# Attention scores of one head at a time over all 128 array rows, with zero-padded q, in place of two heads side by side in two row tiles

## The reference, cut to what matters

```python
h = rms_norm(x, attn_norm)
qa, ka, va, qd, kd, vd = split(h @ w_in)            # 256 x 512 each
qa, ka, qd, kd = rope of each, in 8 heads of 64 columns
out_a = rms_norm(merge_heads(moba_attention(qa, ka, va)))
out_d = rms_norm(merge_heads(dilated_attention(qd, kd, vd)))
x = x + concatenate([out_a, out_d]) @ w_out
x = x + square(relu(rms_norm(x) @ w_up)) @ w_down   # d_ff 4096
# inside the attention, for every head:  scores = q @ k.T * 64 ** -0.5
```

## Time and profile before

| | |
|---|---|
| median of 3 runs | 613.45 us (613.41 to 613.94) |
| the profiled execution's own time | 614.13 us |
| its span in the trace | 612.0 us |
| mean granted TensorE clock | 0.998 |
| PE busy | 600.8 us, 98% |
| DVE, ACT, POOL busy | 62%, 52%, 7% |

### The profile page before, as it was taken

How to read it: one execution, slowest core, us unless ns; L and a number is a source line. 1 busy time by engine, 2 the same in 40 slices (tenths; PEclk the granted TensorE clock), 3 DMA queues, 4 the chain that set the end, 5 groups by cost and what they waited for, 6 DMA issues and landing times.

```text
span 612.0 us, 8795 instructions
## 1 busy us (share of the span) xinstructions
PE 600.8 (98%) x3145; PEld 500.2 (82%) x3145; DVE 378.7 (62%) x576; ACT 316.5 (52%) x534; POOL 44.2 (7%) x42
## 2 busy tenths in 40 slices
PE   7999999999999999999999999999999999999995
PEld 4788787888888888888888788788888888888884
DVE  4854854588675665656388355737976565655734
ACT  5746567656443534534184545764763544535423
POOL 1220140010000000000004010400100000000001
PEclk9999999999999999999999999999999999999999
DMA  8954234328746556465256443422586556466201
GB/s 304 344 206 139 99 116 131 135 73 274 261 156 219 188 168 239 142 232 180 69 189 224 139 137 139 123 84 70 182 297 215 199 155 242 151 198 214 103 0 69
DMA packets 58952, 104.05 MB, mean 170 GB/s; under 512 B 1792, under 2 KB 35376, under 8 KB 58928
## 3 DMA queue, kind: packets, MB, share of 16 engines
q1 hardware_dynamic: 58576, 103.19, 49.8%
q10 hardware_dynamic: 352, 0.55, 0.3%
HBM read 102.69 MB, written 1.05 MB: 170 GB/s over the span
## 4 chain that ended last, share of the span: by engine, by line
PE 94%; DMA 2%; DVE 1%; issue 1%; POOL 1%; ACT 1%; SPq 1%; POOLq 0%; DVEq 0%; ACTq 0%
PE psum L921 19%; PE psum L795 19%; PE psum L797 18%; PE psum L796 18%; PE psum L924 10%; DMA raw<-in_w_in 2%; PE psum L865 2%; PE psum L802 1%; PE psum L856 1%; PE psum L881 1%; PE psum L882 1%; PE psum L901 1%; PE psum L897 1%; PE psum L880 1%; POOL roped L343 1%
## 5 line engine op out<-in xcount | busy, mean ns | idle before, releaser
L529 DVE TENSOR_TENSOR w_lo<-raw,w_hi 128x1024 fp32r<-128x1024 f32 x190 | 231.0, 1251 | 53.0 <-ACT w_hi L385 53.0
L385 ACT CAST w_hi<-raw 128x1024 fp32r<-128x1024 f32 x190 | 188.5, 1047 | 3.7 <-DMA raw<-in_w_in 3.0
L921 PE MATMUL psum<-xt,w_hi 128*128 128x512 f32 x512 | 160.8, 395 | 0.0
L795 PE MATMUL psum<-w_hi,ot_hi 128*128 128x512 f32 x320 | 127.0, 397 | 0.0
L797 PE MATMUL psum<-w_hi,ot_lo 128*128 128x512 f32 x320 | 124.8, 390 | 0.0
L796 PE MATMUL psum<-w_lo,ot_hi 128*128 128x512 f32 x320 | 124.7, 390 | 0.0
L924 PEld LDWEIGHTS psum<-xt,w_lo 128*128 128x128 f32 x512 | 96.2, 188 | 22.4
L924 PE MATMUL psum<-xt,w_lo 128*128 128x256 f32 x512 | 100.6, 278 | 0.0
L921 PEld LDWEIGHTS psum<-xt,w_hi 128*128 128x128 f32 x512 | 80.2, 189 | 2.3
L795 PE MATMUL psum<-w_hi,xt 128*128 128x512 f32 x192 | 79.9, 416 | 1.6 <-DVE w_lo L529 1.0
L476 ACT COPY up_cross<-psum 128x512 f32<-128x512 f32 x32 | 18.8, 587 | 118.9 <-PE psum L924 118.9
(11 more groups left out here) (79 smaller groups left out, 472.5 us busy)
## 6 DMA issues: line engine op xcount, KB each, us to landing
raw<-in_w_up SPq DMA_DIRECT2D x32, 1024.0 KB, 5.5
raw<-in_w_down SPq DMA_DIRECT2D x32, 1024.0 KB, 6.8
raw<-in_w_in SPq DMA_DIRECT2D x22, 1024.0 KB, 5.5
raw<-in_w_out SPq DMA_DIRECT2D x8, 1024.0 KB, 4.8
raw<-in_w_in SPq DMA_DIRECT2D x2, 512.0 KB, 5.1
raw<-in_w_in SPq DMA_DIRECT2D x3, 256.0 KB, 3.6
out<-x SPq DMA_DIRECT2D x3, 256.0 KB, 2.4
x<-in_x SPq DMA_DIRECT2D x2, 256.0 KB, 4.1
```

Source lines behind the costliest of these rows:

```text
L385: act.copy(w_hi[:, slot, part], raw[:, slot, part]).then_inc(hi_done, 1)
L529: dve.tensor_tensor(w_lo[:, slot, part], raw[:, slot, part], w_hi[:, slot, part].bitcast(F32), ALU.subtract).then_inc(split_done, 1)
L795: pe.matmul(out, s_hi, m_hi, start=first, stop=False)
L921: pe.matmul(up_banks[b][:, f, :], w_hi[:, slot, cols[f]], xt[:, k, :, :].rearrange("p a b -> p (a b)"), start=k == 0, stop=False)
```

## The change

Head 2n and head 2n+1 of a pair are no longer computed in two row tiles. The array `q_t` becomes `q_pad`, with two copies of each tile: copy 0 has head 2n's q in partitions 0 to 63 and zeros in the others, copy 1 has head 2n+1's q in partitions 64 to 127 and zeros in the others. Each of the four matmuls of a pair then uses all 128 rows, with `k_t` of both heads as the moving operand, and the zeros cancel the other head's part. They stand in another order: both matmuls of the even head, then both of the odd one. Each ACT copy of q out of `t_bank` becomes two, one for each half of the partitions. DVE sets `q_pad` to zero once at the start, and ACT waits for that once.

```diff
-        q_t = sb("q_t", [4, SEQ])
+        q_pad = sb("q_pad", [2, 4, SEQ])
...
+        zeros_set = sem("zeros_set")
...
                         n = QKT_AT[s]
-                        dst = (q_t, k_t)[n // 2 % 2]
+                        tiles = slice(2 * (n % 2), 2 * (n % 2) + 2)
                         act.wait_ge(qk_turned, l * 8 + n + 5)
-                        act.copy(dst[:, 2 * (n % 2):2 * (n % 2) + 2, :],
-                                 t_bank[:, :].rearrange("p (a b) -> p a b", a=2)).then_inc(qk_copied, 1)
+                        if n // 2 % 2 == 0:
+                            lower, upper = slice(0, HEAD_DIM), slice(HEAD_DIM, P)
+                            if l == 0 and n == 0:
+                                act.wait_ge(zeros_set, 1)
+                            act.copy(q_pad[lower, 0, tiles, :],
+                                     t_bank[lower, :].rearrange("p (a b) -> p a b", a=2))
+                            act.copy(q_pad[upper, 1, tiles, :],
+                                     t_bank[upper, :].rearrange("p (a b) -> p a b", a=2)).then_inc(qk_copied, 1)
+                        else:
+                            act.copy(k_t[:, tiles, :],
+                                     t_bank[:, :].rearrange("p (a b) -> p a b", a=2)).then_inc(qk_copied, 1)
...
             dve.memset(squares[:, 1, 0:BANK], 1.0).then_inc(ones_set, 1)
+            dve.memset(q_pad[:, :, :, :], 0.0).then_inc(zeros_set, 1)
...
                     if hh >= 2:
                         pe.wait_ge(masked, l * N_HEADS + h)
-                    lower, upper = slice(0, HEAD_DIM), slice(HEAD_DIM, P)
                     n = hh // 2
-                    pe.matmul(s_banks[0][:, 0:P], q_t[lower, n, 0:P], k_t[lower, n, 0:P],
-                              start=True, stop=True)
-                    pe.matmul(s_banks[1][:, 0:P], q_t[upper, n, 0:P], k_t[upper, n, 0:P],
-                              start=True, stop=True)
-                    pe.matmul(s_banks[0][:, P:3 * P], q_t[lower, n, P:2 * P], k_t[lower, n, :],
-                              start=True, stop=True).then_inc(scored, 1)
-                    pe.matmul(s_banks[1][:, P:3 * P], q_t[upper, n, P:2 * P], k_t[upper, n, :],
-                              start=True, stop=True).then_inc(scored, 1)
+                    for e in range(2):
+                        pe.matmul(s_banks[e][:, 0:P], q_pad[:, e, n, 0:P], k_t[:, n, 0:P],
+                                  start=True, stop=True)
+                        pe.matmul(s_banks[e][:, P:3 * P], q_pad[:, e, n, P:2 * P], k_t[:, n, :],
+                                  start=True, stop=True).then_inc(scored, 1)
```

## The result

| | before | changed |
|---|---|---|
| median, us | 613.98 (6 runs) | 618.39 (6 runs) |
| lowest to highest | 613.41 to 614.71 | 617.75 to 618.75 |
| ratio | | 1.007, 95% interval 1.0059 to 1.0082 |
| span of the profiled execution | 612.0 | 616.3 |
| PE busy | 600.8 | 605.2 |

The changed kernel is slower by 4.4 us, 0.7%. The forecast was +4.2, and 618.39 lies within its range.

What follows compares the result with a forecast made beforehand. PE was taken to bound the kernel. Pairs +4.3, copies +0.1 and given back −0.2 summed to +4.2 us: 618.3 us for the profiled execution (617.7 on the median), range 615.9 to 619.7, 84%.

Steps and rivals of the forecast that it cites:

- The bound: Whole kernel: PE is busy 600.8 of 612.0 us, so more or less streaming on PE is kernel time.
- The two switches: Scores of each pair: entering and leaving row tiles goes away, saving 0.40 us a pair, 6.4 us in all.
- Streaming: Scores: heads run one after the other, 1.32 us a pair against 1.05; +0.27 a pair, +4.3 us (+3.4 to +5.8).
- the border of up to 0.04: Scores: 0.04 us a pair for entering and leaving full-array float32, counted in the upper bound of 1.41 a pair.
- Copies: Eight q copies on ACT become sixteen; PE gets `t_bank` back later in slot 13 of both layers: +0.1 us (0.0 to 0.3).
- Zeros: Start of the kernel: DVE's zeroing ends at 3.5 us, before its next instruction at 5.63, and costs nothing.
- Given back: PE's waits for probabilities, 0.8 us in all: a slower PE could find them ready, −0.2 us (−0.5 to 0).
- A full-array pass at half the time: Rival, scores: a single head's 256-column pass takes 0.11 us, a pair 0.88; kernel gains 2.7 us, 610.7; 5%.
- Loads exposed between passes of the same rows: Rival, scores: each of 8 passes pays 0.10 us more, +1.1 a pair, +17 us, 631; 3%.
- Hidden: Rival, attention stage: PE's idle takes in 4 us, or the switches are dearer; no change, 613.5 us; 5%.
- The copies as the holder: Rival: q copies hold PE up, 4 a layer by up to 0.5 us each; +4 us more, 621.7; 3%.

Runs made afterwards that it cites:

- merged kernels: Against the changed kernel and its fp32r version: k padded instead of q, both heads' keys in one matmul; 620.93 us in float32, 606.81 us in fp32r.
- head-by-head kernel: Against the kernel before: still two row tiles, but both matmuls of the even head ahead of the odd head's; 614.15 us, ratio 1.0001.

## Why the prediction was right

- *The bound.* PE sets the pace; PE's busy time and the span grew by 4.4 and 4.3. Right.
- *The two switches*, 0.40 us a pair, gone. Right: the idle for "issue" went from 6.0 to 0.7, and the kernel with one head in a row tile (1.04) and the fp32r kernel in row tiles (0.62) fit the same 0.40 with less work inside it. That the array stands idle for 0.09 us on the way in and out agrees with the Trainium skill (TensorEngine Tiling (Array Packing), Key Properties), which says that a change of tiling mode drains TensorE.
- *Streaming*, 1.32 a pair forecast, 1.30 to 1.31 measured in twelve pairs and 1.37 in the four behind a product with v; a 256-column float32 pass takes 0.22 over all rows as in a row tile. Right: +0.25 to +0.26 in most pairs and +0.31 in four, within +0.21 to +0.36. Together they make +4.4 where +4.3 was forecast. The longer first pass in the four was not foreseen; only the border of up to 0.04 in the upper bound made room for it.
- *Copies*, +0.1 for both layers: the transposes of slot 13 are 0.10 later in each, so it was 0.2, within the bounds of 0 to 0.3. The load was 0.29 later where up to 0.15 was forecast, since the second copy overlaps neither neighbour. As an edit of its own it measured 0.1 (614.1 against 614.0), within noise.
- *Zeros*, hidden: they end at 3.71, before 5.63. Right.
- *Given back*, −0.2 forecast, about −0.26 measured, at the sixth pair of each layer. So 4.4 for the pairs, 0.2 for the copies and −0.26 make the 4.3 by which the span grew. The place was not the one named: the idle that the profile puts down to probabilities is 0.8 us in both kernels, and what went was idle for "issue" ahead of the transposes of the probabilities. The 14 pairs between the first and the last, read as 1.05 to 1.11 in the prediction, give 1.05 or 1.06.
- *Rivals.* A full-array pass at half the time: excluded by L910 at 0.22. Loads exposed between passes of the same rows: excluded, L910's load at 45.74 runs under L908's passes; the Trainium skill's rule that loads overlap only where the row group differs (TensorE: Matmul & The Clock Gate, Part 3) does not hold here. Hidden: no, the whole 4.3 us is in the span. The copies as the holder: not on q. But its mechanism is real, and costs 1.1 us an instance in float32, where the copy stands in a slot in which ACT is full; the merged kernels show it.

Luck had a part: that the copies were put on q, whose slots have room, was read off the trace for slots 13, 38 and 40, but I had not seen how near the k slots were to costing something. That the total came so close has chance in it too: the four dearer pairs add 0.2, and 0.26 a pair in place of 0.27 takes 0.2 away. And that the forecast did not hang on the order of the four matmuls was not known either; my expectation for the head-by-head kernel, +7 us, was wrong by all of it.

## What to carry to other kernels

Going in and out of row tiles costs about 0.40 us here, with float32 inside (1.05 us a pair) as with fp32r (0.62); putting two things side by side saves streaming one of them. So compare the second thing's streaming time, all its passes taken together, with the two switches: above it tile (0.65 here), below it pad with zeros (0.23 here). By the same sum a lone small matmul should be padded; that was not run. An added copy on an engine that is half idle is priced by its slot, not by the engine's share: look at who waits for the buffer behind it.

## What the runs showed of the hardware that I had not expected

- Two row tiles work side by side even where the program has all of one tile's matmuls ahead of the other's: 1.06 us a pair against 1.05 interleaved, with the odd head's first matmul ahead of the even head's second in the trace.
- An fp32r matmul of 256 columns over all rows can start 0.05 us after one of 128 (45.58 to 45.63), and the next comes 0.18 later; a pair of them takes 0.23 together.
- ACT overlaps neighbouring instructions by about 0.1 us (0.48 instead of 0.59), but not where the starting partition changes between 0 and 64 (0.59 to 0.61), and at a few other steps (slots 13 and 47) for a reason that is open.
- The first float32 pass of 128 columns behind the passes of 64 columns takes longer: 0.28 us for two passes at 410.18, against 0.21 at 45.63.
